# TensorE's first filling step ahead of the scores in each attention slot

## The reference, cut to what matters

```
# fox: per block of 128 queries and head
s = einsum('bhtd,bhsd->bhts', q[:, :, t0:t1], k[:, :, :t1])
s = s + f_cum[t] - f_cum[s];  p = softmax(where(mask, s, -inf))
out = einsum('bhts,bhsd->bhtd', p, v[:, :, :t1])
# hybrid layers: the same form three times (window 128 with sinks, compressed keys, selected and full window),
# and beside it the delta net: triangular solve per chunk of 64, then a scan over 8 chunks
v_new = u_c - w_c @ state;  o_c = qd_c @ state + qk_c @ v_new
state = state * gl_c + kd_c.T @ v_new
```

## Time and profile before

| | before |
|---|---|
| median of 3 runs | 3070.65 us (3068.67 to 3077.63) |
| profiled execution | 3068.48 us, its span 3067.0 us |
| TensorE, VectorE, ScalarE busy | 94%, 55%, 37% of the span |
| mean granted TensorE clock | 0.956 |

### The profile page before, as it was taken

How to read it: one execution, slowest core, us unless ns; L and a number is a source line. 1 busy time by engine, 2 the same in 40 slices (tenths; PEclk the granted TensorE clock), 3 DMA queues, 4 the chain that set the end, 5 groups by cost and what they waited for, 6 DMA issues and landing times.

```text
span 3067.0 us, 35358 instructions
## 1 busy us (share of the span) xinstructions
PE 2870.2 (94%) x14106; PEld 2297.8 (75%) x14106; DVE 1673.6 (55%) x2910; ACT 1121.2 (37%) x1908; POOL 9.4 (0%) x21
## 2 busy tenths in 40 slices
PE   6878999999998999997998989999999999899998
PEld 4666888867666688884887767888868778678887
DVE  6748756563555665655546755444555477543334
ACT  3433423234554432424424443222334344332223
POOL 0000000000000000000000000000000000000000
PEclk9969999999998999998988999999999899999999
DMA  6324655532221365661230003444432100122222
GB/s 237 130 69 151 199 188 169 190 116 86 72 67 49 108 203 183 193 205 62 96 103 1 1 28 107 140 145 144 147 110 96 70 1 2 55 86 99 97 97 83
DMA packets 92067, 336.19 MB, mean 110 GB/s; under 512 B 10480, under 2 KB 10736, under 8 KB 91776
## 3 DMA queue, kind: packets, MB, share of 16 engines
q1 hardware_dynamic: 86800, 315.40, 31.1%
q10 hardware_dynamic: 3792, 14.31, 1.3%
q0 software_dynamic: 1312, 4.23, 0.5%
HBM read 331.76 MB, written 2.13 MB: 109 GB/s over the span
## 4 chain that ended last, share of the span: by engine, by line
PE 87%; DVE 7%; ACT 4%; DMA 1%; issue 1%; ACTq 0%; DVEq 0%
PE bank L595 22%; PE bank L596 22%; PE bank L597 22%; PE bank L774 2%; PE bank L788 2%; PE bank L763 2%; DVE in_low L1175 1%; DVE hidden L1178 1%; PE bank L1007 1%; PE bank L862 1%; PE bank L612 1%; PE bank L1015 1%; PE bank L613 1%; PE bank L614 1%; PE bank L643 1%
## 5 line engine op out<-in xcount | busy, mean ns | idle before, releaser
L595 PE MATMUL bank<-in_high,weights_high 128*128 128x512 f32 x2160 | 874.0, 405 | 45.8 <-DVE in_low L1175 34.5
L596 PE MATMUL bank<-in_low,weights_high 128*128 128x512 f32 x2160 | 856.0, 396 | 0.0
L597 PE MATMUL bank<-in_high,weights_low 128*128 128x512 f32 x2160 | 855.5, 396 | 0.0
L1085 DVE TENSOR_TENSOR weights_low<-weight_ring,weights_high 128x1024 fp32r<-128x1024 f32 x404 | 494.0, 1223 | 467.0 <-ACT weights_high L1710 467.0
L1710 ACT ACTIVATE weights_high<-weight_ring 128x1024 fp32r<-128x1024 f32 x404 | 424.6, 1051 | 482.7 <-PE bank L597 320.6
L595 PEld LDWEIGHTS bank<-in_high,weights_high 128*128 128x128 f32 x2160 | 414.3, 192 | 183.0 <-issue 55.4
L597 PEld LDWEIGHTS bank<-in_high,weights_low 128*128 128x128 f32 x2160 | 414.3, 192 | 88.9
L596 PEld LDWEIGHTS bank<-in_low,weights_high 128*128 128x128 f32 x2160 | 415.2, 192 | 85.3 <-issue 3.8
L595 PE MATMUL bank<-hidden_split,weights_high 128*128 128x512 f32 x864 | 336.2, 389 | 0.0
L597 PE MATMUL bank<-hidden_split,weights_low 128*128 128x512 f32 x864 | 336.2, 389 | 0.0
L596 PE MATMUL bank<-hidden_split,weights_high 128*128 128x512 f32 x864 | 336.2, 389 | 0.0
(11 more groups left out here) (330 smaller groups left out, 2985.8 us busy)
## 6 DMA issues: line engine op xcount, KB each, us to landing
weight_ring<-stream SPq DMA_DIRECT2D x597, 512.0 KB, 3.4
mixer_out<-cmp ACTq DMA_DIRECT2D x6, 1024.0 KB, 4.8
hidden<-forget_rows POOLq DMA_DIRECT2D x16, 256.0 KB, 3.6
residual<-x ACTq DMA_DIRECT2D x4, 512.0 KB, 12.9
mixer_out<-cmp SPq DMA_DIRECT2D x2, 1024.0 KB, 5.9
out<-mixer_out ACTq DMA_DIRECT2D x4, 512.0 KB, 2.7
constants<-consts ACTq DMA_DIRECT2D x1, 2013.5 KB, 20.9
silu_c<-c ACTq DMA_DIRECT2D x2, 512.0 KB, 4.6
```

The costliest lines, as they stand in the source:

```text
L595: pe.matmul(bank[:, :], WHI[:, z, cols], high, start=(k == 0), stop=False)
L596: pe.matmul(bank[:, :], WHI[:, z, cols], low, start=False, stop=False)
L597: ins = pe.matmul(bank[:, :], WLO[:, z, cols], high, start=False, stop=(k == ktiles - 1))
L1085: v.tensor_tensor(WLO[:, z, :], ring[:, n % RING, :], WHI[:, z, :].bitcast(F32), ALU.subtract).then_inc(*mark("weights_low", "low", n))
```

## The change

On TensorE alone, in both the fox and the hybrid attentions, `fill(d, 0)` is issued at the slot's beginning, ahead of the waits and matmuls of the scores. Nothing is added or removed, and the orders of VectorE, ScalarE, GpSimd and SyncE are as before.

```diff
             for d in range(slots):
+                fill(d, 0)
                 if d < n:
                     begin(d)
                     for z in range(2):
...
                         it, w = items[2 * d + z], items[2 * d + z]["width"]
                         pe.matmul(B[2 + z][:, 0:w], it["q"], it["k"], start=True, stop=True).then_inc(
                             *mark("tensor_attention", *name, "scores", 2 * d + z))
-                fill(d, 0)
                 if 2 <= d <= n + 1:
                     out_free(d - 2)
```

## The result

The changed kernel takes 3196.99 us (median of 4 runs, 3192.08 to 3205.86), the kernel before 3069.66 us (4 runs beside it, 3068.64 to 3077.63): a ratio of 1.0412, 95% interval 1.038 to 1.0444, or **127 us slower**. Slower was forecast, by 85 us. The time lies inside the range for 8 in 10 (3098 to 3200), at its upper end, and outside the range that the first case gave itself (3125 to 3190). The profiled execution took 3192.63 us around a span of 3191.2. In the changed kernel the scores' line is L764 instead of L763.

What follows compares the result with a forecast made beforehand. The prediction took TensorE, busy 94% of the span, to bound the kernel. Fox +29 and two hybrid layers at 28 each (+56) made +85 us on 3070.65, so 3156; range for 8 in 10, 3098 to 3200.

Steps and rivals of the forecast that it cites:

- the first case: Fox and hybrid stages both lose, as summed: +85 us, 3156 us, own range 3125 to 3190; chance .60.
- the rival with the clock: Hybrid attentions: new waits also make the clock fall, 16 falls at 1.6 us, +26, 3182 us; chance .12.
- Fox, +29: Fox attention: seven times 2.7 + 1.6 us, less 3 at the start, plus 2 for clock falls; bounds 15 to 40.
- The wait of r = 3: Fox, slot r = 3: TensorE's product waits for a later eviction, growing from 2.0 to about 4.7 us, seven times.
- that of L595: Fox, slot r = 1: next gemm newly waits 1.6 us for ScalarE's eviction of the bank, seven times.
- p to q: Hybrids: q waits for ScalarE's late copy of p, +2.0 us in a 512-wide slot; five slots, 8 us a layer.
- the rest: Hybrids' 18 other slots: q then q, q then p, rows, tok, kk, xt; together 12 us a layer, 0 to 20.
- The scans' loop of 7.7 us: Hybrid scan slots: loop through VectorE takes 7.7 instead of 6.3 us, +1.4; 8 us a layer over the eight.
- Hybrids hide it: Rival: VectorE and ScalarE work off the delay within a hybrid slot; +25 to +55, middle 3111 us; chance .19.
- Nothing moves: Rival: late maxima stay under other work, only the fox start's wait and cold clock are saved; 3066 us; chance .05.
- faster: Rival: the delta chain sets the hybrids' pace, so F0 starting earlier gives -20, 3050 us; chance .04.
- the 5.11 us chain: Fox, slot r = 2: from the gemm's eviction to TensorE's next product; claimed to have no slack, 3.3 us late.

Runs made afterwards that it cites:

- all_ahead: The changed kernel with VectorE and ScalarE also doing the first filling step ahead of the pair's maxima and exponentials; 3127.68 us, ratio 1.019.
- fox_only: The changed kernel with the new place of F0 kept in the fox attention only, hybrids in the old order; 3095.62 us, ratio 1.0075.
- kept_busy_2: The changed kernel plus five 128x128x128 identity matmuls in each of a hybrid layer's eight kv steps, continuing the bank's accumulation; 3158.09 us, ratio 1.0286.
- hyb_only: The changed kernel with the new place of F0 kept in the hybrid attentions only, fox in the old order; 3174.34 us, ratio 1.0327.
- one_delay: The kernel before plus four small VectorE memsets ahead of the state's clearing, once per hybrid layer; 3107.1 us, ratio 1.0112.
- scans_only: The changed kernel with F0 ahead only in the hybrids' slots from 24 on, the eight scans; 3132.46 us, ratio 1.0188.

## Why the prediction was right, and where it was off

The direction and the range came out, the sum did not by its own mechanism. The upper bounds of the terms added together give 40 + 80 = 120 us, 3191 us; 3197 lies above all of it, and nearer to the rival with the clock (3182) than to the 3156 of the first case. (The range 3125 to 3190 wasn't the terms' bounds half-way, as it says: that would be about 3131 to 3173; 3190 is all upper bounds at once.)

**Direction and mechanism: right.** F0 ahead of the scores takes away the cover of the softmax, and everything that VectorE and ScalarE owe for F0 stands behind it. `all_ahead`, which turns their order too, removes the fox loss, so for fox this cause is shown and not argued. For the hybrids' waits it is read from the traces.

**Fox, +29: measured 25** (`fox_only`). The wait of r = 3 was forecast at 4.7 us and is 4.52; that of L595 at 1.6, seven times, and it is 10.7 / 7 = 1.53. ScalarE's copy was to be 3.35 us behind the gemm's end, and it is 3.4. The first scores' wait of 3.17 us is gone, as said. Waits alone give 17.4 + 10.7 - 3.2 = 24.9 us, so "one or two more" falls of the clock, 2 us of the sum, can't be told from nothing.

**Hybrids, the waits: +56 forecast, 43 found** (21.4 us a layer for 28). p to q is 1.87 for 2.0, four times (6.0 us) for the 8 forecast. Ahead of the scans 16.5 us were found for the 20 forecast (8 for p then q, 12 for the rest), in the scans 4.9 for 8. The scans' loop of 7.7 us could not show, since with the clock at half TensorE takes 10 to 11 us a slot. `kept_busy_2`, at full clock, has slots of 6.5 to 8.0 us, but the added matmuls, 1.3 us a slot, would cover nearly all of the forecast's 1.4; at L1041 between 2630 and 2700 TensorE waited 1.3 us for L1661 (in the changed kernel L1659), in two places, and 1.1 us for another. So the price of the loop at full clock is not settled. Of the signs I had named, "scan waits for the state update" is there with .2 us only, and "slots of 7.7 us" were not seen.

**The clock in the hybrids: the step that failed.** The likeliest case had no fall there, and I gave the rival that had them .12. That the clock falls is what happened, but the rival's price was formed wrongly as well: "16 falls, +26", each 1.6 us as in fox. In the changed kernel's scans the clock is at the lower level for about 60 us a layer, in one stretch or two, and this costs 20 to 30 us. In fox what follows a wait is a gemm of 512-wide matmuls on the full array, and the clock comes back within the period. In the scans it stays down much longer, though TensorE is busy nearly all the time. I had taken the price of a fall from the stage where I could see one. The errors have opposite signs: -4 in fox, -13 in the waits, and some +60 in a term held at zero give 85 + 43 = 128, for the 127 measured. That 127 still fell into the range for 8 in 10 is partly luck: the waits, forecast 17 us too high, made up for a part of the missing 60.

**The other rivals.** "Hybrids hide it" falls with +104 in `hyb_only`. "Nothing moves" and "faster" fall with the +127: the product behind the 5.11 us chain waits 2.5 us longer, so the chain had no slack, and each stage by itself is slower.

**Open.** What in the scans keeps the clock low is not settled. Many of their matmuls use 64 rows or 64 columns of the array (64\*128 and 128\*64 in the rows), and the added ones that hold the clock are 128\*128; shape, count, time and the wait that they fill weren't varied apart. The same scans have the clock back after 13.7 us in `fox_only` and after 44 us in `one_delay`, so the shape alone doesn't explain how long it stays down. Also open is where between .63 and 2.61 us the wait before the scans begins to cost, and why the fox stage of `all_ahead` is shorter than before.

## What to carry to other kernels

When one engine's order is turned, ask what work of that engine was covering a chain on the others, which keep their own order: the loss is the chain less what is left above it, and it can be read from the timeline (here 4.7, 1.6 and 2.0 us forecast for waits that measured 4.52, 1.53 and 1.87). Price each new wait a second time, by the granted clock of the stage that follows it: a stretch that runs at 1.00 with no waits says nothing about how it comes back after one. Where a wait of a few microseconds can't be removed and the windows show the clock falling behind it, matmuls without use that just fit into it are worth a try: here some 8 us of 3070, in an interval of 3 to 12. Three, which overrun the wait by .8 us, left no gain that could be told from none.

## What the runs showed of the hardware

I had not expected a busy TensorE at the lower level for so long: 58.07 of 60 us busy at .51 in the changed kernel, 49.62 of 50 at .56 in `one_delay`, 83.03 of 90 at .50 in `scans_only`. The Trainium skill (TensorE: Matmul & The Clock Gate, Part 1) says that throttled is the default and that activity releases it. The scans that run at 1.00 with added full-size matmuls in them (`kept_busy_2`) agree with this, but the runs don't agree that being busy is by itself enough: in `fox_only` the clock even falls at 2610.9 us in a stretch with 10.62 of 10.90 us busy before it and 13.70 of 13.70 behind it. Nor had I expected that one wait of 2.61 us, 2.1 more than the kernel before has there, costs 18 us a layer. And filling a 2-us wait of the fox attention with two matmuls takes its falls away: .95 becomes 1.00 over 204 us.
